# Rotary queries inside the last input product, later recurrence copies, and DVE eviction of the embedding banks, in a one-layer hybrid encoder trunk

## The reference

```python
q_lat, kv_lat, k_rope_raw, g_mla, u_lru, g_lru, m_mla, m_lru = jnp.split(z, IN_SPLITS, axis=-1)
q = (rms_norm(q_lat, q_a_norm) @ w_q_b).reshape(B, S, N_HEADS, QK_NOPE + QK_ROPE)
q_rope = apply_rope(q_rope, cos[:, :, None, :], sin[:, :, None, :])
kv = (rms_norm(kv_lat, kv_a_norm) @ w_kv_b)
# chunk-causal attention over 16 heads; o * silu(gate) @ w_o
xc = causal_dwconv(u, conv_w, conv_b)
r = sigmoid(blockdiag(xc, w_rg) + b_rg); i = sigmoid(blockdiag(xc, w_ig) + b_ig)
# a = exp(-8 r softplus(-lam)); h = scan(a, sqrt(1 - a^2) * i * xc); h * silu(gate) @ w_o
merged = sigmoid(m_mla) * y_mla + sigmoid(m_lru) * y_lru
x = x + merged @ w_out
x = x + (p @ w_ple) * sigmoid(rms_norm(x, ple_norm) @ w_ple_gate)
```

## Time and profile before

| | |
|---|---|
| median of 3 runs | 2061.48 us (2060.77 to 2062.03) |
| the profiled execution, whole | 2058.73 us |
| its span, first to last instruction | 2056.8 us |
| PE busy | 1995.9 us, 97% |
| POOL / ACT / DVE busy | 900.7 / 719.8 / 655.6 us |
| mean granted PE clock | 0.995 of full |

### The profile page before, as it was taken

How to read it: one execution, slowest core, us unless ns; L and a number is a source line. 1 busy time by engine, 2 the same in 40 slices (tenths; PEclk the granted TensorE clock), 3 DMA queues, 4 the chain that set the end, 5 groups by cost and what they waited for, 6 DMA issues and landing times.

```text
span 2056.8 us, 25476 instructions
## 1 busy us (share of the span) xinstructions
PE 1995.9 (97%) x9070; PEld 1658.3 (81%) x9070; DVE 655.6 (32%) x935; ACT 719.8 (35%) x1249; POOL 900.7 (44%) x683
## 2 busy tenths in 40 slices
PE   7999999999999999999998999899999999999996
PEld 6888888888888888888887788788888888888885
DVE  3100000000454637263427445691010151111344
ACT  7322222222253434443344444422222222333333
POOL 2444444444454544454442322154444454444552
PEclk9999999999999999999999999999999999999998
DMA  6533333333223323242362322353333343234332
GB/s 237 183 118 108 122 122 109 137 122 123 82 86 114 106 84 120 97 143 82 106 150 83 127 76 75 118 197 128 117 122 122 103 180 126 82 103 184 103 102 102
DMA packets 128688, 247.06 MB, mean 120 GB/s; under 512 B 15053, under 2 KB 40309, under 8 KB 120565
## 3 DMA queue, kind: packets, MB, share of 16 engines
q1 hardware_dynamic: 116688, 185.09, 27.6%
q10 hardware_dynamic: 11941, 61.17, 7.8%
HBM read 214.26 MB, written 29.36 MB: 118 GB/s over the span
## 4 chain that ended last, share of the span: by engine, by line
issue 60%; POOL 37%; POOLq 1%; DVE 1%; PE 0%; ACT 0%; DVEq 0%
POOL wlo L359 37%; POOLq L358 1%; POOLq L355 0%; DVE x L1238 0%; PE ps L1249 0%; DVE x L1211 0%; DVE stage L1210 0%; DVE x L1241 0%; POOLq L359 0%; ACT stage L793 0%; DVEq L126 0%; DVE nrm L830 0%; DVE nrm L835 0%; DVE nrm L836 0%; DVE nrm L831 0%
## 5 line engine op out<-in xcount | busy, mean ns | idle before, releaser
L359 POOL TENSOR_TENSOR wlo<-raw,whi 128x512 fp32r<-128x512 f32 x672 | 899.4, 1342 | 1130.6 <-ACT whi L375 1129.8
L375 ACT ACTIVATE whi<-raw 128x512 fp32r<-128x512 f32 x672 | 421.0, 631 | 1169.4 <-PE ps L1249 1107.4
L1249 PE MATMUL ps<-hhi,whi 128*128 128x512 f32 x1408 | 548.7, 390 | 4.8 <-POOL wlo L359 4.8
L1249 PE MATMUL ps<-hlo,whi 128*128 128x512 f32 x1408 | 547.8, 389 | 0.0
L1249 PE MATMUL ps<-hhi,wlo 128*128 128x512 f32 x1408 | 547.8, 389 | 0.0
L1249 PEld LDWEIGHTS ps<-hhi,whi 128*128 128x128 f32 x1408 | 264.3, 188 | 62.0 <-POOL wlo L359 6.9
L1249 PEld LDWEIGHTS ps<-hlo,whi 128*128 128x128 f32 x1408 | 264.3, 188 | 55.0 <-issue 0.2
L1249 PEld LDWEIGHTS ps<-hhi,wlo 128*128 128x128 f32 x1408 | 264.3, 188 | 54.8
L908 DVE TENSOR_TENSOR stage<-ps,stage 128x512 f32<-128x512 f32 x16 | 11.1, 692 | 413.3 <-ACT stage L475 411.9
L1249 PE MATMUL ps<-lhi,whi 128*128 128x512 f32 x256 | 99.7, 389 | 2.5 <-DVE llo L824 2.5
L1249 PE MATMUL ps<-whi,mhi 128*128 128x512 f32 x256 | 99.9, 390 | 0.0
(11 more groups left out here) (253 smaller groups left out, 2442.6 us busy)
## 6 DMA issues: line engine op xcount, KB each, us to landing
raw<-in_w_in SPq DMA_DIRECT2D x88, 1024.0 KB, 5.0
raw<-in_w_o_lru SPq DMA_DIRECT2D x16, 1024.0 KB, 4.9
raw<-in_w_o_mla SPq DMA_DIRECT2D x16, 1024.0 KB, 4.9
raw<-in_w_out SPq DMA_DIRECT2D x16, 1024.0 KB, 4.9
raw<-in_w_ple_gate SPq DMA_DIRECT2D x16, 1024.0 KB, 4.9
sig_scr<-stage ACTq DMA_DIRECT2D x8, 1024.0 KB, 7.1
raw<-in_w_kv_b SPq DMA_DIRECT2D x32, 256.0 KB, 4.0
stage<-sig_scr ACTq DMA_DIRECT2D x8, 1024.0 KB, 4.8
```

The source lines that it names most:

```text
L359: pool.tensor_tensor(wlo[:, k % RING], raw[:, k // RAWC, k % RAWC], whi[:, k % RING].bitcast(F32), ALU.subtract).then_inc(lo_ready, 1)
L375: act.activation(whi[:, c % RING], raw[:, c // RAWC % 2, c % RAWC], ACT.Copy).then_inc(hi_ready, 1)
L1249: return pe.matmul(o, l, r, start=start, stop=stop)
```

## The change

Three things, in one diff.

- **Rotary queries.** The eight chunks of rotary queries move from behind C_M3 into it. The merged stretch has 24 chunks in six blocks of four: merge gate, merge gate, rotary 0, merge gate, rotary 1, merge gate. Both rotary halves use set 1. ACT's `rope_out` and swap stand behind split 11 and split 19 of the stretch, and the second swap goes to `latkv` instead of `stage`. The merge gate's sigmoid and store come last, just ahead of the attention loop; its store now raises `stage_idle`. The weights are loaded in the new order.
- **Recurrence.** ACT's copies to `xchi` move from behind splits 0, 1, 2, 3 to 2, 4, 6, 7, the sigmoids from 6, 7, 10, 11 to 8, 9, 11, 12, and PE's gate pairs from behind chunks 5 and 9 to 7 and 10.
- **Embedding banks.** `ple_out` of groups 0, 1 and 2 is done by DVE, group 3 stays on ACT. Group 0 stands before the mean square and group 1 between it and the Newton steps. Group 1 goes to `sqj` instead of `stage`, so its wait for the first store goes. ACT only issues the stores, later.

The diff, cut to its core:

```diff
@@ -92,8 +92,8 @@
-    C_QR = C_M3 + KD
-    C_ATT = C_QR + 2 * KL
+    C_QR = (C_M3 + 2 * RAWC, C_M3 + 4 * RAWC)
+    C_ATT = C_M3 + KD + 2 * KL
@@ -105,10 +105,10 @@
-    U_QR = (17, 24)
-    U_ATT = (18, 25)
+    U_QR = 24
+    U_ATT = (17, 26)
@@ -306,15 +306,18 @@
+            for n, (what, j) in enumerate((("m", 0), ("m", 1), ("qr", 0), ("m", 2), ("qr", 1), ("m", 3))):
+                r = C_M3 // RAWC + n
                 slot_free(r)
...
@@ -421,16 +421,16 @@
             for t in range(TT):
                 square_x(t)
-            ple_out(0)
             split(RING)
             split(RING + 1)
             root_x()
+            ple_store(0)
             act.wait_ge(x_rstd, 1)
             scale_x(2)
             scale_x(3)
+            ple_store(1)
             split(RING + 2)
             split(RING + 3)
-            ple_out(1)
             act.wait_ge(vec_ready, 1)
             x_turned(0)
@@ -517,12 +517,12 @@
-                    if k < 4:
-                        act.wait_ge(xc_ready, i * 4 + (4 * n + k + 1))
-                        act.activation(xchi[:, k], xc[:, k], ACT.Copy).then_inc(xc_hi, 1)
-                    if k in (6, 7, 10, 11):
-                        t = (6, 7, 10, 11).index(k)
+                    if k in (2, 4, 6, 7):
+                        t = (2, 4, 6, 7).index(k)
+                        act.wait_ge(xc_ready, i * 4 + (4 * n + t + 1))
+                        act.activation(xchi[:, t], xc[:, t], ACT.Copy).then_inc(xc_hi, 1)
+                    if k in (8, 9, 11, 12):
+                        t = (8, 9, 11, 12).index(k)
...
@@ -624,30 +624,27 @@
+            for n in range(KD + 2 * KL):
+                c = C_M3 + n
+                split(c + RING)
+                if n == 0:
                     act.wait_ge(sum_done, 1)
                     squares(latkv, KL)
+                if n == 7:
                     root(TT + 2)
+                if n == 9:
                     latent_hi(latkv, kvhi, KL)
-            act.wait_ge(sum_done, 2)
-            merge_gate_out(1, 0, U_M3)
+                if c == C_QR[0] + KL - 1:
                     rope_out(1, qrf[:, 0:4])
                     act.wait_ge(lat_lo, KL)
                     swap_quadrants(qrf[:, 0:4], latq, 1)
-                    act.wait_ge(sig_stored, 32)
-                    swap_quadrants(qrf[:, 4:8], stage, 2)
+                if c == C_QR[1] + KL - 1:
+                    rope_out(1, qrf[:, 4:8])
+                    act.wait_ge(lat_lo, 2 * KL)
+                    swap_quadrants(qrf[:, 4:8], latkv, 2)
+            act.wait_ge(sum_done, 2)
+            merge_gate_out(1, 0, U_M3, stage_idle)
@@ -856,19 +853,26 @@
+            ple_out(0)
             dve.wait_ge(sumsq_ready, TT)
             mean_square(0, ssq[:, 0, 0:TT])
             signal(root_asked, TT - 1)
+            ple_out(1)
             token_rstd(0, TT)
...
+            ple_out(2)
@@ -1352,10 +1355,10 @@
-                    if k in (5, 9):
+                    if k in (7, 10):
@@ -1385,19 +1388,22 @@
+            for n in range(KD + 2 * KL):
+                c = C_M3 + n
+                j = [j for j in range(2) if C_QR[j] <= c < C_QR[j] + KL]
+                if j:
+                    kq = c - C_QR[j[0]]
+                    if kq == 0:
+                        pe.wait_ge(lat_lo, KL)
+                        claim(1, U_QR + j[0])
+                    chunk(c, features, 1, qlhi[:, kq], qllo[:, kq], kq, KL)
+                else:
+                    chunk(c, features, 0, hhi[:, k], hlo[:, k], k, KD)
+                    k += 1
```

More of the change, by code:

```diff
@@ L107, in trunk_layer @@
     U_M3 = 16
-    U_QR = (17, 24)
-    U_ATT = (18, 25)
-    U_Y = (28, 35)
-    U_O = (32, 39)
+    U_QR = 24
+    U_ATT = (17, 26)
+    U_Y = (27, 36)
+    U_O = (31, 40)
     V_ATTN, V_PLE, V_CB, V_BRG, V_BIG, V_LAM = (KD * n for n in range(6))
@@ L625, in _ @@
                     act.activation(krhi[:], tmp[:, 4], ACT.Copy).then_inc(kr_hi, 1)
-            for k in range(KD):
-                split(C_M3 + RING + k)
-                if k == 0:
+            for n in range(KD + 2 * KL):
+                c = C_M3 + n
+                split(c + RING)
+                if n == 0:
                     act.wait_ge(sum_done, 1)
                     squares(latkv, KL)
-                if k == 7:
+                if n == 7:
                     root(TT + 2)
-                if k == 9:
+                if n == 9:
                     latent_hi(latkv, kvhi, KL)
-            act.wait_ge(sum_done, 2)
-            merge_gate_out(1, 0, U_M3)
-            for k in range(2 * KL):
-                split(C_QR + RING + k)
-                if k == 3:
+                if c == C_QR[0] + KL - 1:
                     rope_out(1, qrf[:, 0:4])
@@ L856, in _, with ple_out @@
             signal(vec_ready)
+            def ple_out(g):
+                s = (g + 1) % 2
+                dve.wait_ge(chunk_used, (g + 1) * KP)
+                for m in range(TT):
+                    ins = dve.tensor_copy(ple_stage(g)[:, m], ps[:, 4 * s + m])
+                ins.then_inc(released[s], 1)
+            ple_out(0)
             dve.wait_ge(sumsq_ready, TT)
@@ L866, in _ @@
             signal(xs_ready)
-            dve.wait_ge(chunk_used, 3 * KP)
-            for m in range(TT):
-                ins = dve.tensor_copy(ple_stage(2)[:, m], ps[:, 4 + m])
-            ins.then_inc(released[1], 1)
+            ple_out(2)
             for k in range(KD):
@@ L1042, in _ @@
             signal(rotated)
-            rotate([qrf[:, 4 + t] for t in range(4)], [stage[:, t] for t in range(4)], 2)
+            rotate([qrf[:, 4 + t] for t in range(4)], [latkv[:, t] for t in range(4)], 2)
             signal(rotated)
-            signal(stage_idle, 16)
             with dve.Fori(0, NG // 2) as i:
@@ L1354, in _ @@
                     chunk(C_LRU + KD + k, features, 0, hhi[:, k], hlo[:, k], k, KD, i, 2 * KD)
-                    if k in (5, 9):
-                        first = 0 if k == 5 else 2
+                    if k in (7, 10):
+                        first = 0 if k == 7 else 2
                         pe.wait_ge(gw_lo, i + 1)
-                        claim(1, U_LRU[1] + (1 if k == 5 else 2), i, 3)
+                        claim(1, U_LRU[1] + (1 if k == 7 else 2), i, 3)
                         gates(first)
@@ L1387, in _ @@
             claim(0, U_M3)
-            for k in range(KD):
-                chunk(C_M3 + k, features, 0, hhi[:, k], hlo[:, k], k, KD)
-                if k == 5:
+            k = 0
+            for n in range(KD + 2 * KL):
[7 more added lines that the diff above has]
+                    chunk(c, features, 1, qlhi[:, kq], qllo[:, kq], kq, KL)
+                else:
+                    chunk(c, features, 0, hhi[:, k], hlo[:, k], k, KD)
+                    k += 1
+                if n == 5:
                     claim(1, U_LAT[1] + 1)
                     square_sum(4, 2)
-            pe.wait_ge(lat_lo, KL)
-            claim(1, U_QR[1])
-            for k in range(KL):
-                chunk(C_QR + k, features, 1, qlhi[:, k], qllo[:, k], k, KL)
-            claim(0, U_QR[0])
-            for k in range(KL):
-                chunk(C_QR + KL + k, features, 0, qlhi[:, k], qllo[:, k], k, KL)
             with pe.Fori(0, NG // 2) as i:
```

26 lines of the change are left out of this document (11 added, 15 removed).

## The result

| | before | after |
|---|---|---|
| median of the runs | 2061.31 us (2060.77 to 2062.03) | 2045.32 us (2041.58 to 2046.27) |
| the profiled execution, whole | 2058.73 us | 2044.64 us |
| its span | 2056.8 us | 2042.8 us |
| mean granted PE clock | 0.995 | 0.996 |

The ratio is 0.9919, 95% interval 0.9902 to 0.9936. The forecast was 2045.4. The median agrees with it to 0.1 us, but not because every term was right: the sites gained more than I had counted, and attention lost some of it in a way I had not counted at all.

What follows compares the result with a forecast made beforehand. PE was taken as the bound, so only its waits and slow clock could be won: 10.2 (entry) + 4.6 (recurrence) + 1.3 (start) = 16.1 us, off 2061.5 gives 2045.4 us; range 2043.2 to 2050.0.

Steps and rivals of the forecast that it cites:

- What bounds the kernel: Whole kernel: PE is busy 1995.9 of 2056.8 us, so time changes only where PE idles or runs slowly.
- Part 1: Entry of attention: moving the rotary queries removes PE's wait for the values, its slow clock and a wlo wait; 10.2 us.
- The cover of 3.1: Entry of attention: set 1 is free 3.1 us before PE asks for it, even with the slower rotation of 12.9.
- The wait of 0.41: Before attention's entry, at 1077.06: PE's wlo wait after ACT's late return goes too, worth 0.57 us with the correction.
- The 2.02 for the clock: Behind the wait for the values: 4.30 us at a granted clock of 0.53 cost 2.02 us, which goes too.
- The table load: ACT, last merge gate's sigmoid: switching tables costs 1.28 us, without the 1.38 us drain the skill adds.
- Part 2: Recurrence: moving ACT's copies and sigmoids and PE's gate pairs removes one wlo wait in each of four passes; 4.6 us.
- Part 3: Start: new embedding evictions bring back only 1.3 us of the waits of 1.05 and 3.12; bounds -0.9 to 2.1.
- A: Recurrence not cured: PE's second claim of set 1 waits for sigmoids held by slow DVE; 2050.0 us, chance 0.10.
- B: Entry of attention: the second rotation still ends late, with 3 us of wait remaining; 2048.4 us, chance 0.06.
- C: First swap starves the ring: PE loses 2.5 us at chunk 16, 2047.9 us; chance 0.04, slower than before 0.02.
- D: Start gives nothing or loses 0.9 us; 2046.7 to 2047.6 us, chance 0.05.

Runs made afterwards that it cites:

- u1: Changed kernel with the rotary queries put back behind the last merge gate, the second swap into stage; 2053.14 us, ratio 0.9965 to the kernel before.
- z2: Kernel before the change, with 27 unread matmuls filling the two longest waits at attention's end; 2059.02 us, ratio 0.9989 to the unfilled kernel before.
- u2: Changed kernel with the recurrence's copies, sigmoids and gate pairs put back to their old places; 2050.02 us, ratio 0.9944 to the kernel before.
- a_again: The changed kernel run once more, unaltered; 2044.17 us, ratio 0.992 to the kernel before.
- u3: Changed kernel with the embedding evictions undone: ACT evicts groups 0 and 1 again, DVE group 2 alone; 2045.5 us, ratio 0.9926 to the kernel before.
- y1: Changed kernel with 12 needless DVE additions behind the second rotation, ahead of qnlo; 2055.82 us in a single execution.
- q1: Changed kernel with only PE's gate pairs back behind chunks 5 and 9, ACT's order left as changed; 2058.29 us in a single execution.

## Why the prediction was right, term by term

- **What bounds the kernel** held: what was won was PE's waits and its slow clock, and where PE has no wait, in the changed recurrence and the changed entry, the time is the same to 0.02 us in every trace that has that code unaltered.
- **Part 1**, forecast 10.2, measured 10.36 in the traces on record. The second rotation was to start at 1069.0 less what parts 2 and 3 had saved; it did at 1062.45, that is 6.6 earlier, against 1.62 + 5.28 = 6.9 saved. The second swap behaved as the old first (4.43 to issue, rotation 6.8 behind the issue's end), as the argument wanted. The first swap took 2.72 to issue instead of 4.11, and its rotation started 8.0 behind its end instead of 6.8; neither mattered. The rotation was slow, 12.8 us, as at the slow end. The cover of 3.1 is 2.4 in one trace and 4.2 in another; the 0.7 missing in the first are the rotation's start, 0.35 late, and the 0.33 between rotation and `qnlo`, which I had left out. The wait of 0.41 is gone too. The 2.02 for the clock was that of one trace: the same old entry costs up to 0.7 more (u1) and 0.5 less (z2).
- The table load: the rows show the split at 1058.92 ending at 1059.55, the load at 1059.57 and the sigmoids at 1060.86. The Trainium skill, "ScalarE: Activation LUTs", section "What ACT_TABLE_LOAD costs", adds a drain of 1.38 us, which is again not there.
- **Part 2**, forecast 4.6, measured 5.28 (5.26 in u2). The mechanism was right in each step, the term of the sum was mis-sized. I had counted a wait as its row plus 0.16. The two matmuls behind it are late too; in the kernel before:

```profile
555.12 0.40 PE L1249 MATMUL ps<-hlo,whi 128*128 128x512 f32 x1
```

  This follows the matmul at 554.78 by 0.34 instead of 0.227. With that 0.11 each of the four waits (1.05, 1.00, 0.98 and 0.98) costs 1.25 to 1.32, together 5.1; the last 0.2 stays open. The same 0.11 belongs to every wait in the sum: two of them bring part 1 to 10.4.
- **Part 3**, forecast 1.3, bounds -0.9 to 2.1, measured 1.62 (first trace), 2.60 (a_again against u3) and, over the eight traces that have the changed start (mean of chunk 12: 59.20) and the three that have the old one (61.29), 2.1. The step that failed: I put 0.4 us of store issue between the scaling and the splits. The row shows the issue at 27.49 beside the scaling, in ACT's queue while ACT works, so the first `hlo` came at 33.03, not 33.65, and `hlo` then set the pace as written. The scaling itself began at 27.49 as I had it (27.4), but by two misses that cancel: the copy of group 1 ended at 26.73 and not 26.1, and the steps behind it took 0.8 us and not 1.2. The other miss is one of scatter. In the old start x was turned at 33.4 to 34.0, held by ACT's eviction; in the new one DVE's copy of group 1 starts when PE has finished that group, so x is turned from 30.4 to 31.8, depending on when PE's clock rose (last matmul of 0.63 us at 12.95 in a_again, at 15.38 in y1) and when the first load landed. And 0.4 is given back at chunk 12, whose `wlo` wait grew from 0.75 to 1.16, where I had let it stay. What the rows did not tell me is that the start of before also ran at half clock, 0.50 from 34.8 to 38.1 us, behind the wait of 3.12. It is worth little: u3 has the old start at full clock there and reaches chunk 12 at 60.91, 0.15 earlier.
- **The sum and the median.** 10.36 + 5.28 + 1.62 = 17.3, and 18.0 with both kernels filled, against my 16.1: too small by 1 to 2 us. The step from the profiled execution to the median was wrong in kind. I took its 2.7 over as a constant. It was half clock at the waits of attention, absent from the one trace that I read and present in most other executions, and the changed kernel's median has some 3 to 4 of it. By the runs: 2058.7 (before without that loss) less 18.0 is 2040.7, plus 2.8 to 4.3 is 2043.5 to 2045.0. So the hit to 0.1 us is luck: a sum 1 to 2 us too small, made up for by a loss of the changed kernel that I had not forecast. (The range's lower end, 2043.2, should by its own words, 2 us below the forecast, have been 2043.4.) Against its second median, 2044.17, the same forecast is 1.2 too high, and 0.5 when it is reckoned from the kernel before beside it.
- **The rivals.** A did not occur, and q1 shows what it would have looked like. B did not: 2.4 us were left. C did not: the first swap's issue took 2.72 us, less than assumed. D did not.

## What to carry to other kernels

Before a step is moved ahead, compute who asks for the bank when, and by how much it is then free; a cover of 2 to 3 us held here because each time on that path came from a row. When a producer's steps are moved later, the consumer's claim must move with them: half of the recurrence's edit alone cost 8.5 us more than none, 1.7 of it by the clock. And read the granted clock at every wait of PE over a microsecond in more than one trace, since a kernel's best profile may lack the loss that most of its runs carry; 27 matmuls that nobody reads, put into PE's idle time, were worth 2.6 us to one kernel and some 3 to 4 to the other.

## What the hardware showed beyond the forecast

- **The same waits, another clock.** Waits of 1.98 and 2.53 us in the same place were followed by 2.4 GHz in the profile of before and by 1.2 GHz in that of after; in u3 the first kept the clock and the second lost it. A stretch at the lower level cost 0.9 to 1.7 us each time (the steps between the values in the table's last columns, u3's 0.9 behind the last matmul aside), and attention plus the rest vary between 943.9 and 948.1 us because of it.
- **DVE beside POOL.** Four products of a rotation take 2.50 us alone and 4.68 and 5.68 beside POOL's subtractions, and twelve additions 12.71 instead of some 7.5 (12 x 2.50 / 4). The Trainium skill, "SBUF — State Buffer", section "SBUF: two separate sides", has a DVE operation with two SBUF inputs and a POOL operation that reads SBUF lock each other out for a whole instruction. The rows agree in size: in y1 four subtractions (7.10 from 1065.86, 1.27 each alone) and four products (6.76 from 1066.76) fill 7.66 us together, and one behind the other they would take 4 x 1.27 + 2.50 = 7.6.
- **Issuing four transfers** took ACT between 2.72 and 4.43 us for the same shapes, and one transfer 0.33, hidden where ACT was computing.
